# Expert layers' head: router products by token tile among the norm's transposes, order copied out first, registers read piece by piece

## The reference, cut to what matters

```python
scores = jax.nn.sigmoid((xf @ router_w).astype(F32))          # 256 x 64
sel_scores = scores + router_b.astype(F32)
grp = sel_scores.reshape(-1, N_GROUPS, N_EXPERTS // N_GROUPS)  # 8 groups of 8
grp_score = jnp.sum(lax.top_k(grp, 2)[0], axis=-1)
_, top_g = lax.top_k(grp_score, TOPK_GROUPS)                   # 4 groups stay
_, topi = lax.top_k(jnp.where(emask, sel_scores, -jnp.inf), TOP_K)   # 6 experts a token
routed = routed_experts(xf, topi, topw, w_gate, w_up, w_down)
shared = (jax.nn.silu(xf @ sh_gate) * (xf @ sh_up)) @ sh_down
```

## Time and profile before

| | us |
|---|---|
| median of 3 runs | 1781.2 |
| lowest, highest | 1780.68, 1783.38 |
| the profiled execution, its own time | 1785.59 |
| its span, first to last instruction | 1783.8 |
| PE busy | 1710.0 (96%) |
| DVE busy | 773.2 (43%) |
| ACT busy | 300.5 (17%) |
| mean granted TensorE clock | 0.986 |

### The profile page before, as it was taken

One profiled execution on the slowest core, in us unless ns is written; L12 is line 12 of the kernel. 1 busy time (PEld: TensorE's weight loads), 2 busy tenths in 40 slices (PEclk: granted clock), 3 DMA queues, 4 the chain that ended last, 5 costly groups with the idle time before them and its releaser, 6 DMA issues.

```text
span 1783.8 us, 25303 instructions
## 1 busy us (share of the span) xinstructions
PE 1710.0 (96%) x10220; PEld 1065.2 (60%) x10220; DVE 773.2 (43%) x1567; ACT 300.5 (17%) x655; POOL 45.7 (3%) x86
## 2 busy tenths in 40 slices
PE   7999999999999999998999999999999999999998
PEld 3876644454444438887946544444444477778884
DVE  2658422222212215797774222222212357735864
ACT  1111401100000003341123100000000231321121
POOL 0100000000000000000000000000000000000000
PEclk9999999999999999999999999999999999999999
DMA  9977699999999996875286999999999876323421
GB/s 402 377 285 312 281 425 423 425 425 425 424 425 425 425 376 233 303 290 212 96 337 258 425 424 425 424 425 425 425 425 425 363 295 244 118 95 121 163 77 49
DMA packets 82093, 576.82 MB, mean 323 GB/s; under 512 B 9132, under 2 KB 11436, under 8 KB 12848
## 3 DMA queue, kind: packets, MB, share of 16 engines
q1 hardware_dynamic: 70992, 494.68, 67.2%
q0 software_dynamic: 10976, 80.43, 11.8%
HBM read 574.01 MB, written 1.06 MB: 322 GB/s over the span
## 4 chain that ended last, share of the span: by engine, by line
PE 65%; DMA 18%; SPq 11%; DVE 3%; issue 2%; ACT 1%; DVEq 0%
PE ps L341 63%; DMA wbuf<-in_moe_gu 10%; SPq L1513 9%; DMA wP<-in_moe_gu 4%; PE ps L345 2%; DMA wbuf<-in_ev_in 2%; DMA wbuf<-in_moe_d 2%; SPq L1529 1%; DVE hma L568 1%; DVE gds L772 0%; DMA wbuf<-in_ada 0%; DVE hma L353 0%; PE ps L466 0%; SPq L1524 0%; ACT slab L348 0%
## 5 line engine op out<-in xcount | busy, mean ns | idle before, releaser
L341 PE MATMUL ps<-slab 128*128 128x128 f32 (+9 forms) x3336 | 560.7, 369 | 7.7 <-issue 2.6
L341 PEld LDWEIGHTS ps<-slab 128*128 128x128 f32 (+4 forms) x3336 | 351.3, 171 | 181.8 <-issue 166.6
L341 PE MATMUL ps<-hma,wbuf 128*128 128x256 f32 (+2 forms) x1616 | 358.0, 380 | 3.2 <-DVE hma L353 1.9
L341 PE MATMUL ps<-wbuf,slab 128*32 128x512 f32 (+3 forms) x1112 | 326.5, 616 | 23.5 <-DMA wbuf<-in_moe_gu 21.6
L341 PEld LDWEIGHTS ps<-hma,wbuf 128*128 128x128 f32 (+1 forms) x1616 | 299.3, 191 | 54.4 <-issue 10.6
L341 PEld LDWEIGHTS ps<-wbuf,slab 128*32 128x32 f32 (+2 forms) x1112 | 102.3, 137 | 172.6 <-issue 129.8
L348 ACT ACTIVATE slab<-ps 128x256 f32<-128x256 f32 (+3 forms) x111 | 50.1, 468 | 864.8 <-PE ps L341 845.3
L1770 DVE TENSOR_TENSOR slab<-ps,slab 128x256 f32<-128x256 f32 x44 | 18.7, 425 | 380.9 <-ACT slab L348 380.9
L568 DVE SCALAR_TENSOR_TENSOR hma<-wbuf,cs,hma 128x1024 f32<-128x1024 f32 x102 | 130.8, 1282 | 12.5 <-DMA wbuf<-in_ada 9.3
L341 PE MATMUL ps<-hma,cst 128*32 128x256 f32 (+3 forms) x424 | 119.2, 486 | 1.6 <-DVE hma L568 1.6
L341 PE MATMUL ps<-cst 128*32 128x512 f32 (+7 forms) x416 | 114.8, 505 | 1.5 <-DVE slab L3240 0.7
(11 more groups left out here) (293 smaller groups left out, 1433.9 us busy)
## 6 DMA issues: line engine op xcount, KB each, us to landing
wbuf<-in_moe_gu SPq DMA_DIRECT2D x90, 1024.0 KB, 24.4
slab<-in_moe_gu SPq DMA_DIRECT2D x64, 1024.0 KB, 22.5
wbuf<-in_ada POOLq DMA_DIRECT2D x60, 1024.0 KB, 5.3
wbuf<-in_moe_d SPq DMA_DIRECT2D x54, 1024.0 KB, 26.1
cst<-in_moe_gu SPq DMA_DIRECT2D x48, 1024.0 KB, 23.8
wbuf<-in_od_in SPq DMA_DIRECT2D x30, 1024.0 KB, 4.9
hma<-in_moe_gu SPq DMA_DIRECT2D x29, 1024.0 KB, 24.2
slab<-in_moe_d SPq DMA_DIRECT2D x23, 1024.0 KB, 16.9
```

Of the source, the lines that this page charges most:

```text
L341: return e.matmul(o, lhsT, rhs, start=start, stop=stop, skip_group_check=skip)
```

## The change

The products of the router's weights with `hT` are made for each token tile by itself (`logits_pe`), tile 0's first half already between the transposes of the norm; the scores, too, are read by ACT and begun by DVE tile by tile. Only half of the gate's rows are made inside the norm, the other half behind the router's products. The shared gate's second half (`m` = 1, eight k) is cut into pieces: k = 0 before `order_pe`, k = 1 and 2 before the gather, k = 3 to 7 behind block 0's gate and up; the residual's transposes go there too. DVE copies the order out before it makes block 0's choice matrix. SP reads a register just ahead of the piece that needs it first. The gate's slot is named later in `freed`.

```diff
@@ -823,9 +823,24 @@
+        def logits_pe(e, l, h, m, f):
+
+            p, u = bank("m_log", l), unit(("m_rt", l), 8, 64)
+            if m == 0 and f == 0:
+                e.wait_ge(*on("landed", ("m_rt", l)))
+            if m == 1 and f == 0:
+                e.wait_ge(*on("m_exp", l, 0))
+            e.wait_ge(*on("n_h", h, m, f))
+            for k in range(4 * f, 4 * f + 4):
+                t = mm(e, p[:, m * 64:m * 64 + 64], hT[:, k, m * 128:(m + 1) * 128], u[:, k, :], k == 0, k == 7, True)
+            if f == 1:
+                t.then_inc(*P.up("m_log", l, m))
+
+        def res_pe(e, kind, last, rows=None, mid=None, logits=None):
             for m in range(2):
                 for f in range(2):
+                    if m == 1 and f == 0 and logits is not None:
+                        logits_pe(e, logits, kind, 0, 0)
...
@@ -834,14 +849,17 @@
                 if m == 0 and rows is not None:
                     ring = banks.ids, banks.i
-                    banks.ids, banks.i = [4, 5], 0
-                    rows_pe(e, *rows)
+                    banks.ids, banks.i = [5, 4], 0
+                    rows_pe(e, *rows, (0,))
+                    fill_bank(e, ("m_log", logits), ("m_exp", logits, 1))
                     banks.ids, banks.i = ring
...
+            if logits is not None:
+                logits_pe(e, logits, kind, 0, 1)
             give_y()
...
@@ -867,12 +885,13 @@
-            if rows is not None:
-                rows_act(e, rows, g_rows, freed_by)
+            if scores is not None:
+                scores_act(e, scores, 0)
+                rows_act(e, rows, g_rows, freed_by, (0,))
+                scores_act(e, scores, 1)
+                rows_act(e, rows, g_rows, freed_by, (1,))
             if ada is not None:
                 ada_row_act(e, ada)
-            if scores is not None:
-                scores_act(e, scores)
...
@@ -1291,11 +1310,11 @@
-            e.wait_ge(*on("m_exp", l))
-            chain(ts(e, r_sc, r_sc, 1.0, None, ALU.add))
-            chain(e.reciprocal(r_sc, r_sc))
-            chain(e.tensor_tensor(r_sel, r_sc, bc(rtb[:, l, :], 2), ALU.add))
             for m in range(2):
+                e.wait_ge(*on("m_exp", l, m))
+                chain(ts(e, r_sc[:, m, :], r_sc[:, m, :], 1.0, None, ALU.add))
+                chain(e.reciprocal(r_sc[:, m, :], r_sc[:, m, :]))
+                chain(e.tensor_tensor(r_sel[:, m, :], r_sc[:, m, :], rtb[:, l, :], ALU.add))
                 for g in range(8):
                     i = e.max(rt8[:, m, g, :], r_sel[:, m, g * 8:g * 8 + 8])
...
@@ -1351,9 +1370,9 @@
-            chosen_dve(e, l, 0)
             e.wait_ge(*on("m_perm0", l))
             e.tensor_copy(order[0:1, l, :], bank("m_cnt", l)[0:1, 128:192]).then_inc(*V.up("m_ord", l))
+            chosen_dve(e, l, 0)
...
@@ -1477,12 +1496,14 @@
-            filled, freed = [rt, gate], [rt, gate]
+            filled, freed = [rt, gate], [rt]
...
                 freed += [("m_w", l, p0 + x, part) for part in (0, 4) for x in range(n)]
+                if q == 0:
+                    freed.append(gate)
...
@@ -1524,12 +1545,13 @@
-                rows_of = [bass.ds(0 if ev.dry else v, 128) for v in
-                           ([128 * x for x in range(p0, p0 + n)] if p0 < FIXED else
-                            [e.value_load(order[0:1, l, x:x + 1], min_val=0, max_val=128 * (NE - 1))
-                             for x in range(p0, p0 + n)])]
+                rows_of = []
                 for part in (0, 4, "d"):
                     for x in range(n):
+                        if part == 0:
+                            v = 128 * (p0 + x) if p0 < FIXED else \
+                                e.value_load(order[0:1, l, p0 + x:p0 + x + 1], min_val=0, max_val=128 * (NE - 1))
+                            rows_of.append(bass.ds(0 if ev.dry else v, 128))
                         src = A["moe_d"][l] if part == "d" else A["moe_gu"][l, part // 4]
                         fill(("m_w", l, p0 + x, part), src[rows_of[x], :])
...
@@ -1595,27 +1617,20 @@
+            for f in range(2):
+                logits_pe(e, l, h, 1, f)
+            P.also("used", ("m_rt", l))
             banks.ids, banks.i = [7], 0
             ada_sum_pe(e, (7, 15)[l])
             banks.ids, banks.i = [6, 4, 5], 0
-            p = fill_bank(e, ("m_log", l), ("m_exp", l))
-            u = unit(("m_rt", l), 8, 64)
-            e.wait_ge(*on("landed", ("m_rt", l)))
-            for m in range(2):
-                for k in range(8):
-                    if k % 4 == 0:
-                        e.wait_ge(*on("n_h", h, m, k // 4))
-                    t = mm(e, p[:, m * 64:m * 64 + 64], hT[:, k, m * 128:(m + 1) * 128], u[:, k, :], k == 0, k == 7)
-            t.then_inc(*P.up("m_log", l))
-            P.also("used", ("m_rt", l))
-            ada_turn_pe(e, (7, 15)[l])
...
+            rows_pe(e, *rows, (1,))
...
@@ -1625,14 +1640,14 @@
-            for m in range(2):
-                p = fill_bank(e, ("m_sh", l, m), ("m_shs", l, m))
-                shared(("m_shg", l), m, p[:, 0:256]).then_inc(*P.up("m_sh", l, m))
-                if m == 1:
-                    P.also("used", ("m_shg", l))
+            p = fill_bank(e, ("m_sh", l, 0), ("m_shs", l, 0))
+            shared(("m_shg", l), 0, p[:, 0:256]).then_inc(*P.up("m_sh", l, 0))
+            ada_turn_pe(e, (7, 15)[l])
+            gate = fill_bank(e, ("m_sh", l, 1), ("m_shs", l, 1))[:, 0:256]
             counts_pe(e, l)
-            residual(((1, 0),))
+            shared(("m_shg", l), 1, gate, range(0, 1))
             order_pe(e, l)
+            shared(("m_shg", l), 1, gate, range(1, 3))
             for half in range(2):
                 gather_pe(e, l, 0, half)
...
@@ -1658,6 +1673,10 @@
                 P.also("m_gu", l, q, 1)
+                if q == 0:
+                    shared(("m_shg", l), 1, gate, range(3, 8)).then_inc(*P.up("m_sh", l, 1))
+                    P.also("used", ("m_shg", l))
+                    residual(((1, 0),))
...
@@ -1716,14 +1735,17 @@
-        def scores_act(e, l):
-            e.wait_ge(*on("m_log", l))
-            afn(e, r_sc, pair(bank("m_log", l)[:, 0:128]), ACT.Exp, scale=-1.0).then_inc(*C.up("m_exp", l))
+        def scores_act(e, l, m):
+            e.wait_ge(*on("m_log", l, m))
+            afn(e, r_sc[:, m, :], bank("m_log", l)[:, m * 64:m * 64 + 64], ACT.Exp, scale=-1.0).then_inc(
+                *C.up("m_exp", l, m))
...
@@ -1731,6 +1753,7 @@
                 if q == 0:
+                    shared(1)
                     e.wait_ge(*on("m_rank", l))
```

More of the change, by code:

```diff
@@ L507, in build, with rows_pe @@
         o_fin = [S(6, 2048)[:, 1536:2048], S(7, 2048)[:, 1536:2048]]
-        def rows_pe(e, kind, cols, ready=None):
-            for f in range(2):
+        def rows_pe(e, kind, cols, ready=None, fs=(0, 1)):
+            for f in fs:
                 p = fill_bank(e, ("g_row", kind, f), ("g_rowc", kind, f))
@@ L517, in rows_pe, with rows_act @@
                 t.then_inc(*P.up("g_row", kind, f))
-        def rows_act(e, kind, dst, freed_by=()):
-            for f in range(2):
+        def rows_act(e, kind, dst, freed_by=(), fs=(0, 1)):
+            for f in fs:
                 e.wait_ge(*on("g_row", kind, f))
@@ L824, in res_dve @@
             turned(1)
-        def res_pe(e, kind, last, rows=None, mid=None):
+        def logits_pe(e, l, h, m, f):
[10 more added lines that the diff above has]
+        def res_pe(e, kind, last, rows=None, mid=None, logits=None):
             for m in range(2):
                 for f in range(2):
+                    if m == 1 and f == 0 and logits is not None:
+                        logits_pe(e, logits, kind, 0, 0)
                     p = fill_bank(e, ("n_t", kind, m, f), ("n_x", kind, m, f), ("n_x" if last else "n_h", kind, m, f))
@@ L1596, in shared_pe, with moe_pe @@
             t.then_inc(*P.up("m_shy", l, j))
-        def moe_pe(e, l, h):
+        def moe_pe(e, l, h, rows):
+            for f in range(2):
+                logits_pe(e, l, h, 1, f)
+            P.also("used", ("m_rt", l))
             banks.ids, banks.i = [7], 0
@@ L1602, in moe_pe, with shared @@
             banks.ids, banks.i = [6, 4, 5], 0
-            p = fill_bank(e, ("m_log", l), ("m_exp", l))
-            u = unit(("m_rt", l), 8, 64)
-            e.wait_ge(*on("landed", ("m_rt", l)))
-            for m in range(2):
-                for k in range(8):
-                    if k % 4 == 0:
-                        e.wait_ge(*on("n_h", h, m, k // 4))
-                    t = mm(e, p[:, m * 64:m * 64 + 64], hT[:, k, m * 128:(m + 1) * 128], u[:, k, :], k == 0, k == 7)
-            t.then_inc(*P.up("m_log", l))
-            P.also("used", ("m_rt", l))
-            ada_turn_pe(e, (7, 15)[l])
-            def shared(key, m, out):
+            rows_pe(e, *rows, (1,))
+            def shared(key, m, out, ks=range(8)):
                 u = unit(key, 8, 256)
                 e.wait_ge(*on("landed", key))
-                for k in range(8):
```

(21 more changed lines are left out.)

## The result

The changed kernel took 1793.2 us (median of 6 runs, 1786.97 to 1795.46) against 1782.0 for the kernel before (6 runs, 1779.22 to 1784.86). The ratio is 1.0057, with a 95% interval of 1.0042 to 1.0072. The prediction was 1776.5, in a range from 1773.2 to 1779.6; it had the wrong sign. The profiled execution is the shortest of the changed kernel's, 1786.97 us with a span of 1785.2.

What follows compares the result with a forecast made beforehand. The prediction took the expert layers to be bound by weight streams at 424 or 425 GB/s that start once the order is there. Gains of 2.5 + 2.2 = 4.7 us took 1781.2 to 1776.5, range 1773.2 to 1779.6.

Steps and rivals of the forecast that it cites:

- Order, DVE's part: DVE's first steps made tile by tile: 1.9 us for both effects, mask complete at 201.05 instead of 202.94.
- third quarter: Router's products on PE: this quarter waits for tile 0's Exp on ACT, starting at 193.85 instead of 192.9.
- Counts: Counts on PE begin when the mask comes, at 201.2 instead of 203.36; total 2.16 us.
- PE's clock falls: Rival: new waits in the head bring PE's clock down, PE 5.6 us late behind block 0, 1786.2; chance 0.05.
- PE's lag behind block 0: Moved work behind block 0's gate and up, less the earlier gather: PE 2.65 - 1.95 = 0.7 us later.
- The thin place's margin: How late the thin place's slot may come without a hole: 3.2 us in layer 0, 3.0 in layer 1.
- thin place: Down piece at 246.3 us (layer 0) and 994.5 us (layer 1), waiting for a slot freed after block 1.
- First issue: SP's first issue behind the order moves from 208.64 to about 204.4, by 4.2 us.

Runs made afterwards that it cites:

- e1_banks: Changed kernel, with counts and gather taking their four banks in the order in which ACT frees them: 1782.6 us, ratio 0.9999 to the kernel before.
- e0_after: The changed kernel again, unedited, for a second profile: 1793.2 us (12 runs), ratio 1.0050 to the kernel before.
- after: The changed kernel itself, in its first measurement and profile: 1793.2 us, ratio 1.0057 to the kernel before.
- e2_warm: Changed kernel with three idle products on constants ahead of the counts: 1786.6 us, ratio 1.0015 to the kernel before.
- e4_dummy6: Kernel before, with seven idle products behind block 0's gate and up in each expert layer: 1791.4 us, ratio 1.0047.
- e5: Kernel before, with three idle products behind block 0's gate and up in each expert layer: 1785.6 us, ratio 1.0009.
- e6: e1_banks with the modulation sum moved ahead of tile 1's router products and the shared gate's pieces moved forward: 1780.6 us, ratio 0.9982 to the kernel before.
- e3_order_early: Kernel before, with only the order's copy ahead of the choice matrix and each register read at its first piece: 1780.7 us, ratio 0.9984.

## Why the prediction was wrong, point by point

- **Order, DVE's part: right.** The reciprocal of half width takes 0.55 us, inside the 0.48 to 0.95 allowed. The mask is complete 1.7 us earlier by the mark (forecast 1.9), and the third quarter waits 0.9 us for ACT (forecast 0.95).
- **Counts: the step that failed.** "The counts begin when the mask comes, at 201.2." I had named two conditions, PE and the mask; the third, the bank, was in the earlier trace rows only as the end of ACT's activations, which PE's work covered. By that row they ended 1.2 us before PE did, so no more than 1.2 of the 2.16 us were to be had. And ACT's turn at `xT` comes behind the second half of the gate's rows, which the change had put later: by the mark it begins 1.2 us later than before (193.96 - 183.97 = 10.0, against 196.50 - 187.67 = 8.8). That ate the rest, and the counts came no earlier at all. Against e1_banks this step cost 2.0 us in layer 0 and 1.7 in layer 1, and the clock on top.
- **The rival "PE's clock falls": it came true in part, with a chance of 0.05.** A new wait did bring the clock down, and PE was 6.5 and 5.3 us late behind block 0, against the rival's 5.6. But the wait was the bank's, which the rival didn't name, and in layer 0 the low clock lay behind the counts (from about 200.7 to 207.5 us, by the stretches of 0.84, 0.50 and 0.81), not ahead of them: the counts came 0.1 us later, not 2.4. That the lateness agrees is luck. Of the 7.0 us between its 1786.2 and the 1793.2 measured, the greater lateness explains 0.6 and the margin below 2.4; the rest is open, and the traces differ in it (the layers land 7.5 us later together in the first profile, 10.7 in e0_after's). Its chance was worked out from pauses of 0.95 and 0.4 us, and layer 0's real one was 2.9; e1_banks has pauses of 0.9 us there and keeps its clock. But in layer 1 of the first profile the clock fell ahead of the counts, behind pauses of 1.7, 1.2 and 0.9 us, and in e1_banks pauses of 1.4, 1.2 and 0.9 at the same place left it at 1.00, so these traces give no length of pause that decides. The Trainium skill (TensorE: Matmul & The Clock Gate, "A second HAM failure mode: psum-queue depth-cycling") speaks of PE idling briefly and often between groups of products as it cycles through PSUM banks, and of what re-warming costs after that; the trace agrees in so far as the clock is 1.00 before the wait for a bank and 0.50 behind it, but in layer 0 it was a single wait.
- **PE's lag behind block 0: half a microsecond short.** Forecast 0.7, in e1_banks 1.23 and 1.22. The gather came 1.65 us earlier instead of 1.95, and the moved work cost 2.9 instead of 2.65.
- **The thin place's margin: the term that was mis-sized most.** I took 3.2 and 3.0 us from the issue's time to landing. In the 14 layers of the seven kernels in which the thin place and not the order decides (after, e0, e1, e2, e4, e5, e6), the last landing is later than before by the slot's lateness less 0.9 to 2.5 us, 1.9 in the mean. That is 1.2 us less than the 3.1. The next section shows why: the time to landing is that of the slowest engine.
- **First issue: right once the head is.** In e1_banks it is 3.8 us earlier, of the forecast 4.2; in e3_order_early the copy and the reads alone give 1.9 (forecast 2.0).

Put together with the banks right: 4.7 us forecast, less 2 x 0.5 for the lag and 2 x 1.2 for the margin, leaves 1.3 a run; e1_banks's landings give 0.5 and its median 0.3. So with the banks right this change would have made no difference that can be measured.

## What the runs showed of the hardware that I had not expected

**A landing says when the slowest DMA engine is done, not how full the queue is.** In e4_dummy6 the pieces land 2.4 to 2.5 us apart as long as the queue is not empty, but the one at 276.2 us lands 3.7 us behind its predecessor, though six more pieces were queued. The stretches around it, columns as in the earlier trace rows:

```profile
270.00:273.00 3.00, 3.00 (x21) 0.78 (x14) 0.69 (x1) 0.00 (x0) 0.00 (x0) 1.00 1.03 431
273.00:276.00 3.00, 3.00 (x17) 1.00 (x15) 0.00 (x0) 0.00 (x0) 0.00 (x0) 1.00 1.00 421
```

The queue of instruction fetches between 272 and 276.2 us (packets, MB, share of 16 engines):

```profile
q8 instruction: 1, 0.02, 1.5%
```

The rate doesn't fall, 431 and 421 GB/s, so nothing was lost. The trace keeps the sixteen updates of each piece's semaphore, though no view prints them, and they tell why. Of the piece at 276.2 us the ninth came at 274.53 and the fifteenth at 274.88, about 2.4 and 2.6 us behind those of the piece before, and only the sixteenth at 276.17. One share of each piece had got 1.3 us behind the others and stayed there. The Trainium skill (DMA: Bandwidth & Descriptors, "Why a DMA increments its semaphore by 16 and not by 1") says that a transfer's engines finish independently and only the last completes it; the trace agrees.

The `instruction` packet beside it, 16 KB that keeps one engine for 1.0 us (it begins at 272.4), is the likely reason. Such packets come about every 21 us, 84 in a run. In the expert streams of the nine traces 57 of 60 such jumps (a landing over 0.7 us late, with three or more pieces under way) stand 1 to 6 us behind one of them, where chance would put about a quarter. Once the stream is dense the next jump is mostly that of the eighth packet further on, 147 to 185 us later, as if they went round eight engines and a jump came whenever the same one is hit again. That the packets cause the jumps is read from this coincidence and wasn't tried.

**This lag is what the margin lacked.** The ninth of the sixteen updates tells when just over half of the shares are in. Times from the issue, layer 0 / layer 1, us:

| | sixteenth update (the landing) | ninth update |
|---|---|---|
| first issue behind the order, idle queue, kernel before | 4.8 / 4.8 | 4.6 / 4.7 |
| thin place, kernel before | 8.0 / 7.8 | 6.4 / 6.1 |
| their difference, the margin | 3.2 / 2.9 | 1.8 / 1.4 |
| margin measured in the seven kernels | 0.9 to 2.1 / 2.1 to 2.5 | 1.6 to 1.75 / 1.4 to 1.5 |

The last row is the slot's lateness less what the layer's last piece comes later, by the same update. By the ninth update every one of the seven kernels gives the margin that the kernel before showed, to 0.2 us. So the room in the stream was there to be read, at 1.8 and 1.4 us; the time to landing overstated it, since the slowest engine lagged by 1.6 and 1.7 us at the thin places already. A hole lets the slow engine catch up: at e4_dummy6's thin piece the sixteenth update is 0.15 us behind the ninth, and within seven pieces a jump of 1.1 to 1.3 us follows, in both layers.

**The clock cost more than the pause that brought it down.** Of the 10.6 us that the banks were worth, the waits themselves are about 4 and the lower clock about 6.6 (e2_warm, with layer 1's early fall in it), while pauses of 0.9 us in layer 0's head (e1_banks) left the clock at 1.00.

## What to carry to other kernels

Before making the producer of a value faster, list all that its consumer waits for, with the bank or buffer it writes to among them, and read from the trace when each would have been ready. The latest of those that the change leaves where they are bounds the gain, and past it the consumer's engine stands idle and may lose its clock. If the consumer must wait, give that engine work there rather than behind it, on the side where others wait for slots. And to judge how late a transfer may come, look at the bytes per microsecond around it, or at the updates in the middle of its sixteen, and not only at its time to landing, which holds the lag of the slowest engine.
